# Strassen-like pairs in a SwiGLU kernel: from three pairs per gate/up chunk at quad starts to four at units 3, 6, 9 and 12, with four remainders per chunk on GpSimd

## What is computed

```
h = rms_norm(x, norm_pre)
a = jax.nn.silu(jnp.einsum('bsd,df->bsf', h, w_gate)) * jnp.einsum('bsd,df->bsf', h, w_up)
y = jnp.einsum('bsf,fd->bsd', a, w_down)
return x + rms_norm(y, norm_post)
```

## Time and profile before

| | before |
|---|---|
| median of 3 runs | 1958.58 us (1954.28 to 1958.92) |
| the profiled execution | 1956.94 us, span 1955.2 us |
| TensorE busy | 1939.0 us (99%), granted clock 0.999 |
| VectorE busy | 1608.9 us (82%) |
| ScalarE busy | 1113.8 us (57%) |
| GpSimd busy | 299.2 us (15%) |
| transfers | 408 MB, mean 209 GB/s |

### The profile page before, as it was taken

One profiled execution on the slowest core, in us unless ns is written; L12 is line 12 of the kernel. 1 busy time (PEld: TensorE's weight loads), 2 busy tenths in 40 slices (PEclk: granted clock), 3 DMA queues, 4 the chain that ended last, 5 costly groups with the idle time before them and its releaser, 6 DMA issues.

```text
span 1955.2 us, 26377 instructions
## 1 busy us (share of the span) xinstructions
PE 1939.0 (99%) x9598; PEld 1644.5 (84%) x9598; DVE 1608.9 (82%) x2082; ACT 1113.8 (57%) x1428; POOL 299.2 (15%) x163
## 2 busy tenths in 40 slices
PE   9999999999999999999999999999999999999998
PEld 7898888888888888888899988788887888888886
DVE  5755479999999878788699996689888999698787
ACT  6544465555655545455788875465555555455454
POOL 1000000111111000000589940000111111100000
PEclk9999999999999999999999999999999999999999
DMA  9645557777777776666455545567777777876665
GB/s 338 229 144 191 183 183 216 214 227 230 234 236 226 232 244 210 208 194 208 135 191 181 186 141 193 164 192 227 225 236 212 218 223 227 249 228 215 191 212 157
DMA packets 136250, 408.11 MB, mean 209 GB/s; under 512 B 13570, under 2 KB 36738, under 8 KB 135618
## 3 DMA queue, kind: packets, MB, share of 16 engines
q1 hardware_dynamic: 134036, 396.83, 64.4%
q0 software_dynamic: 2096, 9.70, 1.3%
HBM read 392.84 MB, written 13.63 MB: 208 GB/s over the span
## 4 chain that ended last, share of the span: by engine, by line
PE 79%; DVE 13%; DMA 4%; issue 2%; ACT 1%; POOL 0%; SPq 0%; DVEq 0%; ACTq 0%; POOLq 0%
PE acc L1856 52%; PE acc L2047 5%; PE acc L2048 5%; PE acc L2046 5%; DVE w_lo L1180 5%; PE acc L1867 4%; PE acc L1869 4%; PE acc L1868 4%; DMA raw<-in_units 4%; DVE gate_sum_lo L1471 2%; DVE parts L1495 1%; DVE gpost L1465 1%; DVE raw L1458 1%; DVE gpost L1452 1%; DVE hT_lo L1436 1%
## 5 line engine op out<-in xcount | busy, mean ns | idle before, releaser
L733 ACT ACTIVATE w_hi<-raw 128x1024 fp32r<-128x1024 f32 x632 | 654.7, 1055 | 671.4 <-DVE raw L1458 309.2
L1180 DVE TENSOR_TENSOR w_lo<-raw,w_hi 128x1024 fp32r<-128x1024 f32 x528 | 631.7, 1221 | 182.7 <-ACT w_hi L733 181.3
L1856 PE MATMUL acc<-w_hi,xT_hi 128*128 128x512 f32 x1112 | 344.5, 391 | 0.9 <-DVE xT_lo L1226 0.6
L1856 PE MATMUL acc<-w_lo,xT_hi 128*128 128x512 f32 x1112 | 342.5, 389 | 0.0
L1856 PE MATMUL acc<-w_hi,xT_lo 128*128 128x512 f32 x1112 | 342.5, 389 | 0.0
L1856 PEld LDWEIGHTS acc<-w_hi,xT_hi 128*128 128x128 f32 x1112 | 207.2, 188 | 47.9 <-DVE w_lo L1180 2.5
L1856 PEld LDWEIGHTS acc<-w_hi,xT_lo 128*128 128x128 f32 x1112 | 208.7, 188 | 43.6
L1856 PEld LDWEIGHTS acc<-w_lo,xT_hi 128*128 128x128 f32 x1112 | 208.7, 188 | 43.6
L633 POOL TENSOR_TENSOR w_lo<-raw,w_hi 128x1024 fp32r<-128x1024 f32 x36 | 97.4, 2705 | 757.1 <-ACT w_hi L733 757.1
L1867 PE MATMUL acc<-xT_hi,w_hi 128*128 128x256 f32 x640 | 181.2, 283 | 0.0
L1869 PE MATMUL acc<-xT_hi,w_lo 128*128 128x256 f32 x640 | 181.1, 283 | 0.0
(11 more groups left out here) (283 smaller groups left out, 3227.4 us busy)
## 6 DMA issues: line engine op xcount, KB each, us to landing
raw<-in_units SPq DMA_DIRECT2D x702, 512.0 KB, 4.2
hid_turned_blocks<-tok SPq DMA_DIRECT2D x22, 512.0 KB, 5.3
tok<-hid_turned_blocks SPq DMA_DIRECT2D x88, 128.0 KB, 5.4
gpost<-in_post POOLq DMA_DIRECT2D x4, 1024.0 KB, 7.4
x<-in_x POOLq DMA_DIRECT2D x4, 512.0 KB, 8.3
c_raw<-in_consts POOLq DMA_DIRECT2D x4, 512.0 KB, 6.9
out<-x SPq DMA_DIRECT2D x8, 256.0 KB, 2.8
xT_raw<-in_xT SPq DMA_DIRECT2D x3, 512.0 KB, 6.9
```

Of the source, the lines that this page charges most:

```text
L733: nc.scalar.activation(w_hi[:, s, :], raw[:, s, :], ACT.Copy, scale=scale).then_inc(hi_ready, 1)
L1180: ins = nc.vector.tensor_tensor(w_lo[:, s, :], raw[:, s, :], w_hi[:, s, :], ALU.subtract)
L1856: last = mm(acc[:, 4 * par + 2 * t + h, :], xs, ws[:, s, h * BANK:(h + 1) * BANK], start=start and ws is w_hi and xs is xh, stop=stop and ...
```

## The change

The x tiles keep their natural order. Fast chunks get pairs at units 3, 6, 9 and 12 (chunk 1 at 6, 9, 12), so a pair can straddle two quads; plain are 0, 1, 2, 5, 8, 11, 14 and 15. GpSimd makes the remainders of 2, 5, 8 and 11 (in chunk 1 of 5, 8 and 11), in chunks 1 to 9. VectorE makes the corner sum first, when the first unit of the pair has landed, and then the three others from it. Both silu move behind unit 2 on ScalarE, all four `close` behind unit 1 on VectorE, `lo_hid` behind unit 5, `hidden` behind unit 7, and `turn_hidden` behind unit 13, that is behind the last pair. The row sums of the pair at unit 3 are made at the end of chunk 1. SP's list is as before. The down projection keeps its pairs, with the new order of sums. Below, in this order: the lists, ScalarE's loop, VectorE's sums and loop, and a wait of TensorE.

```diff
-TILE_ORDER = (0, 2, 3, 1)
+TILE_ORDER = (0, 1, 2, 3)
+FAST_AT = (3, 6, 9, 12)
+def plain_at(i):
+    return [u for u in range(16) if u not in fast_at(i) and u - 1 not in fast_at(i)]
-ASIDE = [(q0 + 4 * i + c, 3) for q0 in (Q_F0, Q_F1) for i in range(2, FFC) for c in (0, 3)]
+ASIDE = [unit(q0 + 4 * i, u) for q0 in (Q_F0, Q_F1) for i in FAST_CHUNKS for u in plain_at(i) if u in (2, 5, 8, 11) and (i > 1 or u > 3)]
...
                 for i in range(1, FFC):
                     q = i * 4 + q0
-                    for s in range(4):
-                        split(q, s, gain + s if i == 1 else None)
-                        if i > 1 and s == 2:
+                    u = 0
+                    while u < 16:
+                        if u in fast_at(i):
+                            split_pair(*unit(q, u), gate_sum(layer, i, u), gate_raw_sum)
+                            u += 2
+                        else:
+                            split(*unit(q, u), gain + u if i == 1 and u < 4 else None)
+                            u += 1
+                        if u == 3:
+                            if i > 1:
+                                act.wait_ge(hid_stored, (FFC * layer + i - 1) * 16)
+                            silu(i - 1, 0)
+                            silu(i - 1, 1)
...
+                        if i > 1 and u == 6:
                             hi_hid(i - 2, 0)
                             hi_hid(i - 2, 1)
...
+                def sum_corner(q, s):
+                    dve.wait_ge(raw_landed[s], landings(q, s) * 16)
+                    b11, b12, b21, b22 = pair_halves(q, s)
+                    nc.vector.tensor_tensor(b12, b11, b12, ALU.add).then_inc(raw_corner_ready, 1)
+                def sum_rest(q, s, n, raw_sum):
...
+                    dve.wait_ge(raw_landed[second[1]], landings(*second) * 16)
+                    dve.wait_ge(raw_corner_ready, n)
...
+                    after(nc.vector.tensor_tensor(t2, corner, b22, ALU.add))
+                    nc.vector.tensor_tensor(t3, t2, b11, ALU.subtract)
+                    nc.vector.tensor_tensor(t4, t2, b21, ALU.add).then_inc(raw_sum_ready, 1)
...
+                    if i > 1:
+                        split(q, 0)
+                        split(q, 1)
                     if i - 1 in FAST_CHUNKS:
                         for t in range(T):
                             wait_sum(dve, t, gu0_ready, i + 11 * layer, q - 1)
                             close(kept, 1 - z, parts, t, 0)
+                            close(kept, 1 - z, parts, t, 1)
...
+                    u = 4 if i == 1 else 2
+                    while u < 16:
+                        if u in fast:
+                            n = gate_sum(layer, i, u)
+                            sum_corner(*unit(q, u))
+                            sum_rest(*unit(q, u), n, gate_raw_sum)
+                            split_pair(*unit(q, u), n, gate_raw_sum, gate_sum_lo[:])
+                            u += 2
+                        else:
+                            if unit(q, u) not in ASIDE:
+                                split(*unit(q, u))
+                            u += 1
+                        if i > 1 and u == 6:
+                            lo_hid(i - 2, 0)
+                            lo_hid(i - 2, 1)
+                        if i > 1 and u == 8:
...
+                            hidden(i - 1, 0)
+                            hidden(i - 1, 1)
...
+                        if u == 14:
+                            turn_hidden(i - 1, 0)
+                            turn_hidden(i - 1, 1)
...
+                        sum_rows(first_raw_rows, 1, rows + 2)
                     if fast:
                         add_parts(closing(layer, i - 1), z, parts)
...
-                    quad(q, xT_hi, xT_lo, 0, z, start=True)
+                        if u == 3:
+                            if i - 1 in FAST_CHUNKS:
+                                pe.wait_ge(closed, closed_count(layer, i - 1))
```

More of the change, by code:

```diff
@@ L72 @@
 SUM_BATCHES = ((2, 4), (4, 6), (6, 8), (0, 2))
-GATE_SUMS = sum(len(fast_quads(i)) for i in FAST_CHUNKS)
+GATE_SUMS = sum(len(fast_at(i)) for i in FAST_CHUNKS)
 LAYER_SUMS = GATE_SUMS + len(FAST_DOWN[0]) + len(FAST_DOWN[1])
@@ L174, in parted, with gate_sum @@
     return 8 * ((b - 1) // 2) + by_tile_halves(t, c) + 1
-def gate_sum(layer, i, c):
-    return LAYER_SUMS * layer + sum(len(fast_quads(n)) for n in range(1, i)) + fast_quads(i).index(c) + 1
+def gate_sum(layer, i, u):
+    return LAYER_SUMS * layer + sum(len(fast_at(n)) for n in range(1, i)) + fast_at(i).index(u) + 1
 def down_sum(layer, j, c):
@@ L947, in ffn @@
                             hi_hid(i - 2, 0)
                             hi_hid(i - 2, 1)
[L949 to L960, removed]
+                        if i == 1 and u in (9, 12):
+                            scale_hi(layer, u // 3 - 2, gain)
@@ L1505, in ffn @@
                     q = i * 4 + q0
-                    fast = fast_quads(i)
+                    fast = fast_at(i)
                     kept = closing(layer, i - 2)
-                    for s in range(3):
-                        split(q, s, gain + s if i == 1 else None)
+                    if i > 1:
+                        split(q, 0)
+                        split(q, 1)
                     if i - 1 in FAST_CHUNKS:
@@ L1525, in ffn @@
                         lo_rows(rows + 1, xs_lo[:], gate_raw_sum.rearrange("p (a c) -> p a c", c=BANK), xs_hi[:])
[L1526 to L1537, removed]
@@ L1549, in ffn @@
[L1549 to L1559, removed]
@@ L1560, in ffn @@
[L1560 to L1572, removed]
-                        end_sums(q + 3, gate_raw_sum)
@@ L2076, in plain_units @@
                     for t in range(T):
-                        last = unit_by_token(s, hi, lo, k0 + s, z, t, False, s == 3 and (stop is not None or pause == t),
+                        last = unit_by_token(s, hi, lo, k0 + s, z, t, start, s == 3 and (stop is not None or pause == t),
                                              resumed=resumed)
@@ L2087, in ffn @@
                 x_quads(q0, b, y_par, par, gu0_ready, pool)
-                rows = (1 + len(SUM_BATCHES)) * layer
+                rows = (X_ROWS + len(SUM_BATCHES)) * layer
                 for i in range(1, FFC):
@@ new lines, in ffn @@
+                    while u < 16:
+                        if u == 3:
+                            if i - 1 in FAST_CHUNKS:
+                                pe.wait_ge(closed, closed_count(layer, i - 1))
+                            else:
+                                pe.wait_ge(hid_ready, i * 2 + 22 * layer)
+                        if i == 1 and u == 4:
+                            pe.wait_ge(x_scaled, len(RESCALED) * layer + 1)
+                        if u in fast:
+                            n = FAST_AT.index(u)
+                            pe.wait_ge(rows_lo_ready, rows + (1 if n else X_ROWS))
+                            s_hi, s_lo = (xs_hi[:, n - 1, :], xs_lo[:, n - 1, :]) if n else (xs_first_hi[:], xs_first_lo[:])
+                            fast_pair(*unit(q, u), gate_sum(layer, i, u), z, xT_hi, xT_lo, u, s_hi, s_lo, gate_sum_lo[:],
+                                      u == fast[0], u == fast[-1])
+                            u += 2
+                        else:
+                            plain_units(q + u // 4, (u % 4,), xT_hi, xT_lo, u - u % 4, z, gu0_ready if u == 15 else None,
+                                        start=u == 0)
+                            u += 1
```

160 lines of the change are left out of this document (72 added, 88 removed).

## The result

The changed kernel takes 2136.43 us (median of 4 runs, 2132.52 to 2138.99) against 1958.19 us for the kernel before beside it. The ratio is 1.0913, with a 95% interval from 1.089 to 1.0936: 9% slower, 178 us more. The forecast was 2175.

The account below looks back on a forecast made before the run. TensorE bounds the kernel before; VectorE's cycle the changed one: 39.4 + 9.6 + 0.9 + 3.7 = 53.6 us per chunk, 12.1 more, 97 over eight. With chunks 1 and 10, 109 per layer, 218 in all: 2175 us, range 2055 to 2240.

Parts of the forecast that it names:

- The gain of TensorE: One more pair in nine chunks and two layers saves TensorE 54 matmuls, 12.2 us; a chunk then needs 40.8 us.
- VectorE's own work: VectorE's operations in a fast chunk, without stands and waits: 39.4 us, against 38.2 before.
- The port: GpSimd remainders and VectorE operations with two SBUF operands exclude each other: four stands, 9.6 us per fast chunk.
- the stand: VectorE's operation blocked by one GpSimd remainder: taken as 2.4 us, bounds 0 and 2.4.
- The store: Late hidden-value store delays the next chunk's loads; VectorE idles 0.9 us for unit 0 and 3.7 for unit 3.
- the landing times: Store lands after 5.3 us; fetches wait for it; units 2 and 3 land 6.6 us after their loads.
- VectorE's wait for the corner of unit 3: VectorE stands 3.7 us per chunk until unit 3 has landed; bounds 1.3 and 5.
- The idle time ahead of units 0 and 1: At the start of a chunk VectorE idles 0.9 us until w_hi of unit 0 is there.
- Chunk 1 and chunk 10: Chunk 1 takes 8 us more (50 against 42.2); chunk 10 takes 4 more, from chunk 9's late store.
- The port alone: Rival: the late turn is absorbed and only GpSimd's stands cost; 47.6 us per chunk, 2071 us, chance 12%.
- the store alone: Rival: GpSimd's remainders fall into VectorE's waits, only the late store costs; 44.0 us per chunk, 2009 us, chance 8%.
- The faster case: Rival: TensorE stays the bound, with VectorE's stands and waits at most 1.4 us per chunk; 1944.7 us, chance 5%.

Follow-up runs that it names:

- experiment 5: The changed kernel with GpSimd clearing w_lo of units 2, 5, 8, 11 by memset (no subtraction) and turn_hidden behind unit 10: 1948.1 us, ratio 0.9969.
- Experiment 9: The changed kernel with no GpSimd remainders (VectorE makes all) and turn_hidden behind unit 10: 2018.4 us, ratio 1.0332.
- experiment 11: The kernel before with only the new order of the four sums, corner first: 1955.9 us, ratio 1.0009.
- experiment 4: The changed kernel with GpSimd clearing w_lo of units 2, 5, 8, 11 by memset in place of the subtraction, so without reading: 2001.6 us, ratio 1.0243.
- experiment 2: The changed kernel with turn_hidden moved up to directly behind hidden (behind unit 7): 2083.9 us, ratio 1.0658.
- experiment 8: The kernel before with turn_hidden moved behind the remainder of the last pair's sums: 2008.3 us, ratio 1.0286.

## Why the prediction was right, point by point

**The gain of TensorE** (12.2 us): right as a count, and it appears only in experiment 5: 7 us in the medians, and in the trace 6.0 us for the eight chunks of layer 0 (331.9 less 325.9).

**VectorE's own work** (39.4 us per chunk): right. Experiment 5 has 39.5 busy per chunk. Experiment 9, with neither stand nor late store, has chunks of 44.9 us for 39.4 and four remainders, 44.0. Four sums in the new order take 0.1 us more per pair than the 2.63 us of the earlier trace rows, which was costed at nothing; experiment 11 shows that it costs nothing in the kernel before.

**The port** (9.6 us per chunk, 168 in all with chunk 1): right mechanism, right order, too large. The four stands measured 2.1, 2.2, 2.1 and 2.2 us, 8.6 per chunk; over the kernel 148 by rows, and without them the kernel is 135 us faster (experiment 4). The term that was mis-sized is the stand: I had taken 2.4, GpSimd's whole remainder. The rows had the difference: VectorE ends 0.55 us behind GpSimd, and its operation takes 0.68 alone, so 0.13 of GpSimd's time is not lost. Here GpSimd ends 2.35 us after `lo_hid` begins, and 2.35 + 0.55 - 0.68 = 2.2.

**The store** (4.6 us per chunk idle, 82 with chunk 10): right mechanism, mis-sized by 30 us. It measured 52.5 (experiment 2); by the two traces some 36 of them in chunks 2 to 9, 2.2 per chunk, and the rest in chunks 1 and 10. The step that failed is the landing times: the store lands after 3.3 us (the median of part 6 of the new page, 5.3 before and 5.1 in experiment 2), so the load of unit 2 went out at 444.6, and ScalarE took it at 449.83, 5.2 us later, not 6.6. VectorE's wait for the corner of unit 3, 3.7 us in the forecast, was nothing: its `close` was done when the corner sum began at 451.09, the unit had landed, and the sum then stood for GpSimd. Where no such stand hides it, in experiment 4, the wait is 0.28 us for unit 3 and 0.60 for unit 4. The idle time ahead of units 0 and 1 was 2.0 in this chunk (1.6 to 4.4 in the others), not 0.9.

**Chunk 1 and chunk 10** (8 and 4): `add_parts` of chunk 1 starts at 342.5 in place of 331.0, 11.5 later; behind chunk 9 some 4 us are left in layer 0 and 8 in layer 1. With 8 x 9.25 = 74 for the chunks between: about 90 per layer, 180 in all. So chunk 1 was put too low by 3.5 us and this made up for a small part of what the two terms above were too high.

**The rivals.** The port alone was put at 2071 and measured 2083.9 (experiment 2 leaves it alone), the store alone at 2009 and measured 2001.6 (experiment 4). Neither holds by itself, and their costs add up, as the forecast had them do. The faster case needed stands and waits under 1.4 us per chunk; they are 10.6. The stated 57 us as upper end of a chunk is more than its own terms give (39.4 + 10.5 + 0.9 + 5 = 55.8). GpSimd did not starve: in the chunk shown it got its turn within 1.4 us, when the operation in front was done.

**The signs named in advance.** The chunk of 49 to 57 us, the operations of 3 us and SP's waiting for the store at the fetches (41.3 us in 20 waits) came. Three signs did not. TensorE is busy 93% of the whole, not under 90; it is under 90 in the eight chunks alone (351.1 of 406.0, 86%). VectorE did not wait before the corner of unit 3. And TensorE waited little for unit 2 (9.0 us in 14 waits for GpSimd's remainders) and much ahead of the pairs (91.9 us in 69), whose remainders VectorE brought late. So the place at which TensorE stands was not the one described; VectorE's cycle, from which the time was worked out, was.

## What to carry to other kernels

Before work goes from VectorE to GpSimd, count on VectorE's list the operations with two SBUF operands that will be ready while GpSimd reads: here each remainder of 1.14 us given away cost 2.1 us, and taking all back gained 69 us. A GpSimd operation belongs beside VectorE work that reads PSUM or one SBUF operand, and it must not be ready earlier than that work, or it takes the port first. In a strict queue, a store placed ahead of loads can pass on the delay of what it waits for: in the kernel before, 1.2 us of transposes moved 6.6 us down VectorE's list cost 53 us in 18 chunks (experiment 8).

## What I had not expected of the hardware

The granted clock fell in short stretches, and behind waits of TensorE of 2 to 3 us; the forecast had reckoned with stands of 5. Two stretches of chunk 2, TensorE's wait of 2.12 us (to 366.03) in the first:

```profile
364.00:368.00 4.00, 1.97 (x7) 1.67 (x8) 4.00 (x5) 3.07 (x3) 0.70 (x1) 0.90 0.23 72
368.00:372.00 4.00, 4.00 (x13) 3.13 (x13) 4.00 (x3) 0.00 (x0) 2.92 (x1) 0.67 0.62 199
```

The matmuls from 367.7 to 370.3 start 0.43 us apart in place of 0.23, seven of them, the level of 1.2 GHz, and from 370.7 on 0.23 again, that of 2.4 GHz. The clock did not fall behind every such wait: in the chunk from 441.59 TensorE waited up to 2.2 us for the remainders ahead of pairs, and the granted clock of the chunk is 1.00. The mean over the kernel is 0.987, against 0.999 before. It is not the bound: experiment 2 ran at 0.984 and was 52 us faster.

And a lone `memset` of the same 128x1024 elements takes GpSimd 0.96 us against 2.41 for the subtraction, and lengthened none of the VectorE operations beside which it ran.
